# A Hymba block: the subtractions of the token pairs' mixing on GpSimd, and the second pair's scaling one group later

## The chip, the cores and the metric

The kernel runs on one core of a Trainium2 chip. The metric is the device time of one execution in microseconds (us). TensorE (PE) multiplies matrices, VectorE (DVE), ScalarE (ACT) and GpSimd (POOL) work elementwise, SyncE (SP) issues DMAs; GpSimd issues some as well. Each engine runs its own instructions in order and waits on semaphores for the others.

## What is computed

For x of 2048 tokens by 1024, in float32:

```python
h = _rmsnorm(x, norm1_w[layer])
proj = h @ w_in[layer]
qa, ka, va, qb, fb, ib, gb = jnp.split(proj, SPLIT_POINTS, axis=-1)
ya = _swa_sink_attention(qa, ka, va, q_norm_w[layer], k_norm_w[layer], attn_sinks[layer])
yb = _hgrn2(qb, fb, ib, gb, lower_bounds[layer], hgrn_gnorm_w[layer])
x = x + (jnp.concatenate([ya, yb], axis=-1) @ w_out[layer]).astype(x.dtype)
h = _rmsnorm(x, norm2_w[layer])
gate, up = jnp.split(h @ w_gate_up[layer], 2, axis=-1)
x = x + ((jax.nn.silu(gate) * up) @ w_down[layer]).astype(x.dtype)
```

`_hgrn2` is a gated linear recurrence over chunks of 64 tokens for four heads; its state between chunks is decayed and added to.

## The kernel before

Every product in float32 is made of three passes over a high and a low part (`three_passes`, L243 to L251): ScalarE copies a weight tile from its stage to `w_hi`, VectorE subtracts that from the stage for `w_lo` (L924).

The first phase (`build_phase_a`) takes the tokens in four blocks of 512. In a block the projections come in chunks of weight columns: KV, QA0, QA1, F0, F1, Q01, I01, G01, F23, Q23, I23, G23, and then WO0 to WO3 for the output projection. A chunk of 256 columns in token order has four groups (numbered 0 to 3) of 24 matmuls each; F and Q chunks have one group for each 128 columns. Two PSUM banks `pj` take turns, so that a group waits until the one before the last has been read. For the WO chunks VectorE reads it, by adding it to the residual tile `x_res` (L988).

The order of all other work is written by hand in `block_steps` (L73 to L143): `after(chunk, group, steps...)` hangs steps behind a group, and every engine walks the same list `STEPS` and does its own part of each step. For HGRN head h the steps are `ha`, `hb`, `hc` (gates), `kt`, `ds` (the update of the state, on VectorE at L1084 and L1088, whose last output is `a_carry`), `att`, `o` (TensorE, L902 and L907; waits for the state) and `on1` to `on3`, `yt` (norm and transposes; `on1` has a power on GpSimd, L513). `split_hi` and `split_lo` are the weight split of a later chunk.

The second phase multiplies the feed-forward matrices by a Strassen-like scheme, which wants seven combinations of each pair of token tiles, `hc` in DRAM. For the first half of the tokens these combinations, the *mixing*, are made in the last block of the first phase (block 3), from the rows of `x_mid` that earlier blocks have stored. A pair p of four is one step `("mix", p, 0)`, the scaling of two tiles of 128x1024 by the norm (L219), and one step `("mix", p, 1)`, four subtractions of 128x512 (L224 to L229). Both are VectorE's. There is one buffer `mix_x` and one `mix_t` for all pairs.

SyncE's queue holds the weight loads of all chunks (L444) and, at two places of that loop and behind it, `store_mixed` (L232 to L240; three stores, each waiting for its part on the semaphore `mixed`) and `load_mix` (L455 to L458), which waits until the pair before is stored. Pair 0 is stored and pair 1 loaded behind the load of G23 and ahead of that of WO0; pair 1 is stored and pair 2 loaded behind the load of WO1 and ahead of that of WO2; the rest comes behind all of them.

GpSimd's queue holds, beside the powers, the residual tiles: at the last group of each WO chunk it stores `x_res` to `x_mid` (L529, waits for ScalarE's squares), waits for that store, and loads the residual of a chunk two further on (L524).

Of the kernel before, what the change touches and what calls it, by code (L numbers as in the profile page):

```python
# [21 lines left out]
ALU = mybir.AluOpType  # L22
# [50 lines left out]
def block_steps():  # L73

    at = {}

    def after(name, group, *steps):
        at.setdefault((name, group), []).extend(steps)

    after("KV", 3, ("vmix",))
    after("QA1", 0, ("qn1", 0))
    after("QA1", 1, ("qn1", 1))
    after("QA1", 2, ("qn1", 2), ("qn2", 0))
    after("QA1", 3, ("qn1", 3))
    after("F0", 0, ("qn2", 1), ("split_hi", CHUNK_AT["Q01"]), ("split_lo", CHUNK_AT["Q01"]), ("qn2", 2))
    after("F1", 0, ("qn2", 3))
    after("Q01", 0, ("qT", 0), ("qT", 1), ("qT", 2), ("qT", 3), ("kT",))  # L90
    after("Q01", 1, ("sc", 0), ("sm1", 0), ("sm1", 1))
    after("I01", 0, ("ha", 0), ("split_hi", CHUNK_AT["G01"]))
    after("I01", 1, ("sm2", 0), ("sm2", 1), ("sc", 1), ("split_lo", CHUNK_AT["G01"]))
    after("I01", 2, ("pt", 0), ("pt", 1), ("sm1", 2), ("sm1", 3), ("hb", 0))
    after("I01", 3, ("sm2", 2), ("sm2", 3), ("pv", 0), ("sc", 2))
    after("G01", 0, ("pt", 2), ("pt", 3), ("sm1", 4), ("sm1", 5), ("xload",), ("hc", 0), ("ha", 1))
    after("G01", 1, ("sm2", 4), ("sm2", 5), ("pv", 1), ("split_hi", CHUNK_AT["F23"]), ("split_lo", CHUNK_AT["F23"]))
    after("G01", 2, ("pt", 4), ("pt", 5), ("sc", 3), ("att", 0), ("kt", 0), ("sm1", 6), ("sm1", 7), ("hb", 1))
    after("G01", 3, ("ds", 0, 0), ("ds", 0, 1), ("sm2", 6), ("sm2", 7), ("pv", 2), ("hc", 1))
    after("F23", 0, ("pt", 6), ("pt", 7))  # L100
    after("F23", 1, ("pv", 3), ("o", 0), ("on1", 0), ("kt", 1), ("ha", 2), ("sq", 0))
    after("Q23", 0, ("on2", 0), ("on3", 0), ("hb", 2), ("split_lo", CHUNK_AT["I23"]), ("ds", 1, 0), ("ds", 1, 1), ("att", 1))
    after("Q23", 1, ("yt", 0), ("hc", 2), ("sq", 1))
    after("I23", 0, ("o", 1), ("on1", 1), ("ha", 3))
    after("I23", 1, ("on2", 1), ("on3", 1), ("split_lo", CHUNK_AT["G23"]), ("kt", 2), ("sq", 2))
    after("I23", 2, ("yt", 1), ("att", 2), ("sq", 3))
    after("I23", 3, ("hb", 3),)
    after("G23", 0, ("ds", 2, 0), ("ds", 2, 1), ("hc", 3), ("n1a",))
    after("G23", 1, ("o", 2), ("on1", 2), ("kt", 3), ("n1b", 0), ("n1b", 1))
    after("G23", 2, ("on2", 2), ("ds", 3, 0), ("ds", 3, 1), ("att", 3))  # L110
    after("G23", 3, ("on3", 2), ("o", 3), ("on1", 3), ("yt", 2), ("n1b", 2), ("on2", 3), ("on3", 3), ("n1b", 3))
    after("Q23", 1, ("mix", 0, 0))
    after("I23", 1, ("mix", 0, 1))
    after("I23", 3, ("mix", 1, 0))
    after("G23", 0, ("mix", 1, 1))
    for n in range(CHUNK_AT["WO0"], NW):
        after(chunk_name(n), 1, ("split_lo", n + 1))
    after("WO0", 2, ("mix", 2, 0), ("mix", 2, 1))
    after("WO1", 3, ("mix", 3, 0), ("mix", 3, 1))
    after("WO0", 0, ("xT", 0))  # L120
    after("WO0", 1, ("xT", 1))
    after("WO0", 2, ("xT", 2))
    after("WO1", 0, ("xT", 3))
    after("WO1", 2, ("xT", 4))
    after("WO2", 0, ("xT", 5))
    after("WO2", 2, ("xT", 6))
    after("WO3", 0, ("xT", 7))

    placed = [step for group in at.values() for step in group if step[0].startswith("split")]
    steps = []  # L130
    for n in range(NW):
        first_steps = [part for part in (("split_hi", n + 1), ("split_lo", n + 1)) if part not in placed]
        for g in range(chunk_groups(n)):
            if (chunk_name(n), g) == ("WO0", 0):
                first_steps.append(("yt", HG - 1))
            if g == 0 and (chunk_groups(n) < TT or chunk_name(n) == "WO0"):
                steps += first_steps
            steps.append(("proj", n, g))
            steps += at.pop((chunk_name(n), g), [])
            if g == 0 and not (chunk_groups(n) < TT or chunk_name(n) == "WO0"):  # L140
                steps += first_steps
    assert not at, at
    return steps  # L143
# [71 lines left out]
def mix_tokens(dve, x, t, rs, at, n2w, mixed, part):  # L215

    if part == 0:
        for two in range(2):
            last = dve.scalar_tensor_tensor(out=x[:, two, :], in0=x[:, two, :], scalar=rs[:, at + 4 * two:at + 4 * two + 1], in1=n2w[:], op0=ALU.mult, op1=ALU.mult)  # L219
            if two == 0:  # L220
                last.then_inc(mixed, 1)
    else:
        dve.drain()
        dve.tensor_tensor(t[:, 0, :], x[:, 1, 0:512], x[:, 0, 0:512], ALU.subtract)  # L224
        dve.drain()
        dve.tensor_tensor(x[:, 1, 0:512], x[:, 1, 512:D], x[:, 1, 0:512], ALU.subtract).then_inc(mixed, 1)
        dve.tensor_tensor(t[:, 1, :], x[:, 1, 512:D], t[:, 0, :], ALU.subtract)
        dve.drain()
        dve.tensor_tensor(t[:, 2, :], t[:, 1, :], x[:, 0, 512:D], ALU.subtract).then_inc(mixed, 1)  # L229
# [24 lines left out]
def build_phase_a(nc, ctx, dram, x_mid, hc, kept):  # L254
# [159 lines left out]
    mid_ready = signal("mid_ready", 1, 1)  # L414
    mix_in, n2w_in, rs_ready = sem("a_mix_in"), sem("a_n2w_in"), sem("a_rs_ready")
    mixed, hc_stored = sem("a_mixed"), sem("a_hc_stored")
    pool_waited, dve_waited = sem("pool_waited"), sem("dve_waited")
    pool_set, dve_set, act_set = sem("pool_set"), sem("dve_set"), sem("act_set")

# [65 lines left out]
    def _(pool):  # L485
# [35 lines left out]
        for b in range(NB):  # L521
# [9 lines left out]
            for step in STEPS:  # L531
# [3 lines left out]
                if kind == "vmix":  # L535
                    if b == NB - 1:
                        wait(mid_ready.sem, 2)
                        pool.drain()
                        pool.tensor_tensor(kept.rs[:, 0:8], mid_ms[:, 0:8], neg_half[:, 0:8], ALU.pow).then_inc(rs_ready, 1)

                    wait(kv_ready.sem, kv_ready.upto(b, TT))
                    pool.drain()
                    pool.tensor_copy(v_even[CHUNK:P, 0, :], v_even[CHUNK:P, TT, :])
                    pool.drain()
                    pool.tensor_copy(v_even[0:CHUNK, 0:TT, :], v_nat[0:CHUNK, :, :])
                    pool.drain()
                    pool.tensor_copy(v_even[CHUNK:P, 1:TT + 1, :], v_nat[CHUNK:P, :, :]).then_inc(v_even_ready.sem, 1)
                elif kind == "qn1":
                    t = step[1]
                    power(q_rs[:, t, :], q_ss[:, t, :], SLOTS, q_ms_ready, q_rs_ready, q_ms_ready.upto(b, t + 1))  # L550
                elif kind == "sc" and step[1] == 1:

                    wait(sink_less_ready.sem, sink_less_ready.upto(b, 2))
                    pool.drain()
                    pool.memset(penalty[:], 0.0)
                elif kind == "xload":

                    wait(kT_full.sem, kT_full.upto(b, 1))
                    if b < NB - 1:
                        load_block(b + 1)  # L560
                    load_res(0)
                    load_res(1)
                elif kind == "on1":
                    h = step[1]
                    power(o_rs[:], o_ss[:], TT, o_ms_ready, o_rs_ready, o_ms_ready.upto(b, h + 1))
                elif kind == "n1a":
                    power(x_rs[:], ss[:], TT, ms_ready, x_rs_ready, ms_ready.upto(b, 1))
                elif kind == "proj" and chunk_name(step[1]).startswith("WO") and step[2] == TT - 1:
                    c = step[1] - len(CHUNKS)
                    store_res(c)  # L570


                    wait(xr_stored[c % 2], b * 32 + 16 * (c // 2 + 1))
                    if c < 2:
                        load_res(c + 2)
# [343 lines left out]
    def _(dve):  # L919
# [54 lines left out]
        for b in range(NB):  # L974
            use = 0
            for step in STEPS:
# [130 lines left out]
                    low_part(yH_lo[h][:], tr[use % 2][:], gnw[:, 0:1], yH_hi[h][:], yH_ready)  # L1107
                elif kind == "n1a":
                    mean_square_x(b)
                elif kind == "mix":  # L1110
                    p, part = step[1:]
                    if part == 0:
                        if p == 0:
                            dve.wait_ge(rs_ready, 1)
                            dve.wait_ge(n2w_in, 16)
                        dve.wait_ge(mix_in, 16 * (p + 1))
                    mix_tokens(dve, mix_x, mix_t, kept.rs, p, n2w, mixed, part)
                elif kind == "n1b":
                    scale_x(b, step[1])
                elif kind == "xT":  # L1120
# [738 lines left out]
```

## Time and profile before

| | us |
|---|---|
| median of 3 runs | 2197.1 |
| lowest and highest | 2196.92, 2197.79 |
| the profiled execution, its time | 2197.5 |
| its span | 2195.7 |
| TensorE busy | 2139.9 |
| VectorE busy | 1337.5 |
| ScalarE busy | 904.7 |
| GpSimd busy | 132.6 |

The span is that of the recorded instructions; the time has 1.8 us more around it. Busy times are sums over the span. A row of the timeline has the start from the beginning of the span, the duration, the engine, the line, what is written and read, and in brackets how long the engine had been idle and what released it. The first phase ends at about 900 us, its last block starts at about 672 us.

### The profile page before, as it was taken

Reading aid. Unit: us, or ns where it says so; the run is one execution under the profiler, and the core shown is the slowest. Engines: PE = TensorE matmul, PEld = TensorE weight load, DVE = VectorE, ACT = ScalarE, POOL = GpSimd, SP = SyncE. Lnnn points to the kernel's source line nnn. Section 1 sums busy time; section 2 is a strip of 40 time slices with the busy share of each in tenths; the row PEclk is TensorE's granted clock in tenths of the full one; section 3 lists DMA queues with packets and bytes.
Section 4 is the critical chain, followed back from the end, with each engine's and each line's share of the span. In section 5 each row is a group of like instructions: output and inputs, shape, how many; then the busy total and the mean of one; then the engine's idle time right before and its main releaser. Section 6 shows DMA issues by size and latency. Waiting matters only on the chain.

```text
span 2195.7 us, 30926 instructions
## 1 busy us (share of the span) xinstructions
PE 2139.9 (97%) x12376; PEld 1856.1 (85%) x12376; DVE 1337.5 (61%) x1967; ACT 904.7 (41%) x1575; POOL 132.6 (6%) x138
## 2 busy tenths in 40 slices
PE   7999999999999998799999999999999999999999
PEld 7889988998899888788888888888888888888887
DVE  4675367636753677567777667777777764444432
ACT  4774377437733762433323334333233332222221
POOL 2101110120012000100000000000000000000000
PEclk9999999999999999899999999999999999999999
DMA  3322232223223326634445335554444575645532
GB/s 138 136 78 91 102 136 78 97 97 139 75 97 105 136 82 237 229 117 141 156 152 187 101 115 187 177 191 140 164 155 146 181 253 175 214 166 179 186 132 91
DMA packets 156271, 316.22 MB, mean 144 GB/s; under 512 B 9504, under 2 KB 96800, under 8 KB 140128
## 3 DMA queue, kind: packets, MB, share of 16 engines
q1 hardware_dynamic: 144864, 265.74, 35.5%
q0 software_dynamic: 11264, 48.50, 6.1%
q8 instruction: 98, 1.61, 0.3%
q14 instruction: 45, 0.37, 0.1%
HBM read 230.85 MB, written 83.36 MB: 143 GB/s over the span
## 4 chain that ended last, share of the span: by engine, by line
PE 58%; DMA 0%; issue 0%; DVE 0%; POOLq 0%
PE b_bank_A L248 4%; PE b_bank_A L249 4%; PE b_bank_A L250 4%; PE b_bank_B L249 4%; PE b_bank_C L249 4%; PE b_bank_B L248 4%; PE b_bank_C L248 4%; PE b_bank_C L250 4%; PE b_bank_B L250 4%; PE b_hx_bank L1614 3%; PE b_hx_bank L1615 3%; PE b_hx_bank L1613 3%; PE b_bank_D L248 2%; PE b_bank_D L249 2%; PE b_bank_D L250 2%; PE b_hx_bank L1558 1%
## 5 line engine op out<-in xcount | busy, mean ns | idle before, releaser
L248 PE MATMUL a_pj<-a_w_hi,a_hT_hi 128*128 128x256 f32 x896 | 259.5, 290 | 1.7 <-issue 1.7
L249 PE MATMUL a_pj<-a_w_lo,a_hT_hi 128*128 128x256 f32 x896 | 253.6, 283 | 0.0
L250 PE MATMUL a_pj<-a_w_hi,a_hT_lo 128*128 128x256 f32 x896 | 253.6, 283 | 0.0
L1501 ACT ACTIVATE b_s_hi<-b_s_stage 128x1408 fp32r<-128x1408 f32 x56 | 77.4, 1382 | 300.1 <-PE b_hx_bank L1615 149.8
L924 DVE TENSOR_TENSOR a_w_lo<-a_w_stage,a_w_hi 128x2048 fp32r<-128x2048 f32 (+1 forms) x64 | 137.9, 2155 | 72.8 <-ACT a_w_hi L587 72.8
L248 PEld LDWEIGHTS a_pj<-a_w_hi,a_hT_hi 128*128 128x128 f32 x896 | 171.9, 192 | 6.7 <-issue 4.4
L249 PEld LDWEIGHTS a_pj<-a_w_lo,a_hT_hi 128*128 128x128 f32 x896 | 172.0, 192 | 0.0
L250 PEld LDWEIGHTS a_pj<-a_w_hi,a_hT_lo 128*128 128x128 f32 x896 | 171.8, 192 | 0.0
L248 PE MATMUL b_bank_A<-b_h_hi_B,b_w_hi 128*128 128x512 f32 x352 | 137.6, 391 | 0.0
L248 PE MATMUL b_bank_B<-b_h_hi_T,b_w_hi 128*128 128x512 f32 x352 | 137.3, 390 | 0.0
L250 PE MATMUL b_bank_A<-b_h_hi_B,b_w_lo 128*128 128x512 f32 x352 | 137.2, 390 | 0.0
L249 PE MATMUL b_bank_A<-b_h_lo_B,b_w_hi 128*128 128x512 f32 x352 | 137.2, 390 | 0.0
L250 PE MATMUL b_bank_B<-b_h_hi_T,b_w_lo 128*128 128x512 f32 x352 | 137.0, 389 | 0.0
L249 PE MATMUL b_bank_B<-b_h_lo_T,b_w_hi 128*128 128x512 f32 x352 | 137.0, 389 | 0.0
L1631 DVE TENSOR_TENSOR b_w_lo<-b_mixed_w,b_w_hi 128x1024 fp32r<-128x1024 f32 x88 | 107.5, 1222 | 22.1 <-ACT b_w_hi L1462 22.1
L1613 PE MATMUL b_hx_bank<-b_t_hi,b_s_hi 128*128 128x512 f32 x308 | 119.8, 389 | 0.0
L1614 PE MATMUL b_hx_bank<-b_t_lo,b_s_hi 128*128 128x512 f32 x308 | 119.8, 389 | 0.0
L1615 PE MATMUL b_hx_bank<-b_t_hi,b_s_lo 128*128 128x512 f32 x308 | 119.8, 389 | 0.0
L587 ACT ACTIVATE a_w_hi<-a_w_stage 128x2048 fp32r<-128x2048 f32 (+1 forms) x64 | 115.6, 1806 | 4.7 <-DMA a_w_stage<-w_whole 4.7
L1631 DVE TENSOR_TENSOR b_s_lo<-b_s_stage,b_s_hi 128x1408 fp32r<-128x1408 f32 x56 | 91.0, 1625 | 33.8 <-ACT b_s_hi L1501 32.7
L1522 ACT ACTIVATE b_s<-b_bank_C 128x512 f32<-128x512 f32 x44 | 26.4, 599 | 200.5 <-PE b_bank_C L250 200.5
L1538 ACT ACTIVATE b_gate<-b_u 128x512 f32<-128x512 f32 x44 | 27.8, 632 | 195.8 <-DVE b_u L1777 195.8
(280 smaller groups left out, 5526.9 us busy)
## 6 DMA issues: line engine op xcount, KB each, us to landing
a_w_stage<-w_whole SPq DMA_DIRECT2D x56, 1024.0 KB, 4.8
b_gu_stage<-w_gu SPq DMA_DIRECT2D x44, 1024.0 KB, 5.1
b_s_stage<-a_sums SPq DMA_DIRECT2D x56, 704.0 KB, 4.2
a_sums<-b_a SPq DMA_DIRECT2D x88, 256.0 KB, 5.5
a_sums<-b_gate SPq DMA_DIRECT2D x66, 256.0 KB, 4.1
b_hx<-hc POOLq DMA_DIRECT2D x13, 1024.0 KB, 5.3
b_w_blocks<-w_dn SPq DMA_DIRECT2D x11, 1024.0 KB, 4.7
a_x_res<-x_pad POOLq DMA_DIRECT2D x16, 512.0 KB, 5.4
```

The lines of the kernel that those rows point to most:

```text
L248: pe.matmul(out, stationary[0](k), moving[0](k), start=(k == 0 and not adds), stop=False, skip_group_check=adds)
L249: pe.matmul(out, stationary[0](k), moving[1](k), start=False, stop=False, skip_group_check=adds)
L250: last = pe.matmul(out, stationary[1](k), moving[0](k), start=False, stop=(k == ends), skip_group_check=adds)
L587: act.activation(w_hi[s][:, :, 0:cols], w_stage[s][:, :, 0:cols], ACT.Copy).then_inc(w_hi_ready.sem, 1)
L924: dve.tensor_tensor(w_lo[s][:, :, 0:cols], w_stage[s][:, :, 0:cols], w_hi[s][:, :, 0:cols].bitcast(F32), ALU.subtract).then_inc(w_lo_ready ...
L1501: act.activation(f.s_hi[n % 2][:], f.s_stage[n % 2][:], ACT.Copy).then_inc(f.s_hi_ready, 1)
L1522: act.activation(f.s5[:], f.bank["C"][:], ACT.Copy).then_inc(f.s5_ready, 1)
L1538: act.activation(f.gate[1][:], f.u2[:], ACT.Silu).then_inc(f.silu_ready[1], 1)
L1613: pe.matmul(out, s_hi[:, k, :], t_hi, start=(k == 0 and not adds), stop=False, skip_group_check=adds)
L1614: pe.matmul(out, s_hi[:, k, :], t_lo, start=False, stop=False, skip_group_check=adds)
L1615: last = pe.matmul(out, s_lo[:, k, :], t_hi, start=False, stop=(k == PAIRS_FF - 1), skip_group_check=adds)
L1631: dve.tensor_tensor(out, full, hi.bitcast(F32), ALU.subtract).then_inc(ready, 1)
```

## The change

The four subtractions of each pair in the last block of the first phase become GpSimd's, with a drain between them; GpSimd waits for the scaling by a new semaphore `mix_scaled`. The step of pair 0's subtractions goes from behind group 1 of I23 to behind group 0, pair 1's scaling from behind group 3 of I23 to behind group 0 of G23, at the end of that list, and pair 1's subtractions from behind group 0 of G23 to behind group 3. Pairs 2 and 3 keep their places. The mixing of the second half of the tokens, in the second phase, stays VectorE's.

```diff
--- before.py
+++ after.py
@@ -110,9 +110,9 @@
     after("G23", 2, ("on2", 2), ("ds", 3, 0), ("ds", 3, 1), ("att", 3))
     after("G23", 3, ("on3", 2), ("o", 3), ("on1", 3), ("yt", 2), ("n1b", 2), ("on2", 3), ("on3", 3), ("n1b", 3))
     after("Q23", 1, ("mix", 0, 0))
-    after("I23", 1, ("mix", 0, 1))
-    after("I23", 3, ("mix", 1, 0))
-    after("G23", 0, ("mix", 1, 1))
+    after("I23", 0, ("mix", 0, 1))
+    after("G23", 0, ("mix", 1, 0))
+    after("G23", 3, ("mix", 1, 1))
     for n in range(CHUNK_AT["WO0"], NW):
         after(chunk_name(n), 1, ("split_lo", n + 1))
     after("WO0", 2, ("mix", 2, 0), ("mix", 2, 1))
@@ -219,6 +219,7 @@
             last = dve.scalar_tensor_tensor(out=x[:, two, :], in0=x[:, two, :], scalar=rs[:, at + 4 * two:at + 4 * two + 1], in1=n2w[:], op0=ALU.mult, op1=ALU.mult)
             if two == 0:
                 last.then_inc(mixed, 1)
+        return last
     else:
         dve.drain()
         dve.tensor_tensor(t[:, 0, :], x[:, 1, 0:512], x[:, 0, 0:512], ALU.subtract)
@@ -414,6 +415,7 @@
     mid_ready = signal("mid_ready", 1, 1)
     mix_in, n2w_in, rs_ready = sem("a_mix_in"), sem("a_n2w_in"), sem("a_rs_ready")
     mixed, hc_stored = sem("a_mixed"), sem("a_hc_stored")
+    mix_scaled = sem("a_mix_scaled")
     pool_waited, dve_waited = sem("pool_waited"), sem("dve_waited")
     pool_set, dve_set, act_set = sem("pool_set"), sem("dve_set"), sem("act_set")
 
@@ -560,6 +562,17 @@
                         load_block(b + 1)
                     load_res(0)
                     load_res(1)
+                elif kind == "mix" and step[2] == 1:
+                    x, t = mix_x, mix_t
+                    pool.drain()
+                    pool.wait_ge(mix_scaled, step[1] + 1)
+                    pool.tensor_tensor(t[:, 0, :], x[:, 1, 0:512], x[:, 0, 0:512], ALU.subtract)
+                    pool.drain()
+                    pool.tensor_tensor(x[:, 1, 0:512], x[:, 1, 512:D], x[:, 1, 0:512], ALU.subtract).then_inc(mixed, 1)
+                    pool.drain()
+                    pool.tensor_tensor(t[:, 1, :], x[:, 1, 512:D], t[:, 0, :], ALU.subtract)
+                    pool.drain()
+                    pool.tensor_tensor(t[:, 2, :], t[:, 1, :], x[:, 0, 512:D], ALU.subtract).then_inc(mixed, 1)
                 elif kind == "on1":
                     h = step[1]
                     power(o_rs[:], o_ss[:], TT, o_ms_ready, o_rs_ready, o_ms_ready.upto(b, h + 1))
@@ -1107,14 +1120,13 @@
                     low_part(yH_lo[h][:], tr[use % 2][:], gnw[:, 0:1], yH_hi[h][:], yH_ready)
                 elif kind == "n1a":
                     mean_square_x(b)
-                elif kind == "mix":
-                    p, part = step[1:]
-                    if part == 0:
-                        if p == 0:
-                            dve.wait_ge(rs_ready, 1)
-                            dve.wait_ge(n2w_in, 16)
-                        dve.wait_ge(mix_in, 16 * (p + 1))
-                    mix_tokens(dve, mix_x, mix_t, kept.rs, p, n2w, mixed, part)
+                elif kind == "mix" and step[2] == 0:
+                    p = step[1]
+                    if p == 0:
+                        dve.wait_ge(rs_ready, 1)
+                        dve.wait_ge(n2w_in, 16)
+                    dve.wait_ge(mix_in, 16 * (p + 1))
+                    mix_tokens(dve, mix_x, mix_t, kept.rs, p, n2w, mixed, 0).then_inc(mix_scaled, 1)
                 elif kind == "n1b":
                     scale_x(b, step[1])
                 elif kind == "xT":
```

## Rows read from the trace of the kernel before

**Rows 1.** The head of the page, and its chain that ended last.

```profile
span 2195.7 us, 30926 instructions
...
PE 58%; DMA 0%; issue 0%; DVE 0%; POOLq 0%
```

**Rows 2.** TensorE's waits from 780 to 1000 us: us in total, times, longest.

```profile
PE a_hb L902 <- DVE a_carry L1088: 7.7, 1, 7.7
```

**Rows 3.** Timeline of VectorE, last block: start, us, instruction, idle time before it.

```profile
811.54 0.69 DVE L224 TENSOR_TENSOR a_mix_t<-a_mix_x 128x512 f32<-128x512 f32 x1
...
817.80 0.69 DVE L1035 TENSOR_TENSOR a_k_end<-a_t_b 128x512 f32<-128x512 f32 x1
823.02 2.48 DVE L219 SCALAR_TENSOR_TENSOR a_mix_x<-a_mix_x,rs,a_n2w 128x1024 f32<-128x1024 f32 x2 [4.54 <-DMA a_mix_x<-x_mid]
...
829.01 0.35 DVE L1088 SCALAR_TENSOR_TENSOR a_carry<-a_state,a_decay,a_tr 128x128 f32<-128x128 f32 x1
...
834.77 2.29 DVE L924 TENSOR_TENSOR a_w_lo<-a_w_stage,a_w_hi 128x2048 fp32r<-128x2048 f32 x1
...
838.26 0.69 DVE L1098 TENSOR_TENSOR a_y_nat<-a_hb,a_o_rs 128x512 f32<-128x512 f32 x1 [1.12 <-POOL a_o_rs L513]
...
856.67 2.47 DVE L219 SCALAR_TENSOR_TENSOR a_mix_x<-a_mix_x,rs,a_n2w 128x1024 f32<-128x1024 f32 x2
```

**Rows 4.** Timeline of TensorE, last block.

```profile
817.58 1.16 PE L895 MATMUL a_tr<-a_i_nat,a_k_nat 64*128 64x128 f32 x16
...
829.50 2.04 PE L902 MATMUL a_hb<-a_i_nat,a_att_m 128*128 128x128 f32 x8 [7.70 <-DVE a_carry L1088]
...
843.46 1.16 PE L902 MATMUL a_hb<-a_i_nat,a_att_m 128*128 128x128 f32 x8 [0.37 <-DVE a_att_m L1080]
...
862.43 0.39 PE L248 MATMUL a_pj<-a_w_hi,a_yA_hi 128*128 128x256 f32 x1 [0.38 <-DVE a_x_res L988]
...
877.47 0.39 PE L248 MATMUL a_pj<-a_w_hi,a_yA_hi 128*128 128x256 f32 x1 [0.39 <-DVE a_x_res L988]
```

**Rows 5.** Stretches: us, busy of PE, PEld, DVE, ACT, POOL, granted clock, DMA, GB/s.

```profile
385.00:403.00 18.00, 15.89 (x150) 14.56 (x149) 13.30 (x27) 5.95 (x23) 4.47 (x2) 1.00 0.17 59
...
822.00:829.50 7.50, 0.00 (x0) 0.03 (x1) 5.54 (x12) 2.86 (x4) 0.00 (x0) 0.74 0.96 371
829.50:834.00 4.50, 4.50 (x27) 3.94 (x28) 4.26 (x7) 0.50 (x4) 0.00 (x0) 0.50 0.02 5
```

**Rows 6.** GpSimd's groups, shapes apart: busy us, mean ns of one.

```profile
L513 POOL TENSOR_TENSOR a_q_rs<-a_q_ss,a_neg_half 128x10 f32<-128x10 f32 x16 | 38.5, 2408 | 66.6 <-DVE a_q_ss L994 66.3 <-issue 0.3
...
L547 POOL COPY a_v_even<-a_v_nat 64x512 f32<-64x512 f32 x4 | 2.5, 613 | 0.5
```

**Rows 7.** Timeline of GpSimd, block 1 and last block.

```profile
390.26 2.98 POOL L513 TENSOR_TENSOR a_x_rs<-a_ss,a_neg_half 128x4 f32<-128x4 f32 x1 [18.22 <-DVE a_ss L928]
...
806.09 1.24 POOL L513 TENSOR_TENSOR a_o_rs<-a_o_ss,a_neg_half 128x4 f32<-128x4 f32 x1 [18.11 <-DVE a_o_ss L1094]
...
847.11 1.01 POOL L513 TENSOR_TENSOR a_o_rs<-a_o_ss,a_neg_half 128x4 f32<-128x4 f32 x1 [8.89 <-DVE a_o_ss L1094]
863.51 0.81 POOL L529 DMA_DIRECT2D x_mid<-a_x_res  x1 [15.40 <-ACT a_junk L640]
869.24 0.75 POOL L524 DMA_DIRECT2D a_x_res<-x_pad  x1 [4.92 <-DMA x_mid<-a_x_res]
```

**Rows 8.** Timelines of SyncE's queue and of ScalarE, last block.

```profile
814.40 0.36 SPq L240 DMA_DIRECT2D hc<-a_mix_t  x1
818.25 0.36 SPq L458 DMA_DIRECT2D a_mix_x<-x_mid  x1
818.66 0.93 SPq L444 DMA_DIRECT2D a_w_stage<-w_whole  x2
...
826.00 1.91 ACT L587 ACTIVATE a_w_hi<-a_w_stage 128x2048 fp32r<-128x2048 f32 x1 [3.32 <-DMA a_w_stage<-w_whole]
```

**Rows 9.** DMA issues of the page: count, size, median us to landing.

```profile
a_x_res<-x_pad POOLq DMA_DIRECT2D x16, 512.0 KB, 5.4
```

## The prediction

> **What bounds the kernel now.** I read the head of the page first: the profiled execution has a span of 2195.7 us and took 2197.5 us, 0.4 above the median of the runs (2197.1), and the chain that ended last runs over TensorE (PE) [rows 1]. So another engine's work counts only where TensorE stands still for it. The list of TensorE's waits from 780 us on has one large entry in the last block: 7.7 us for `a_carry`, the state update of HGRN head 2 [rows 2]. VectorE's timeline says why that update was late [rows 3]. VectorE finished the step `hb` of head 3 at 818.5 (row 817.80), then came pair 1's scaling: it waited 4.54 us for its tokens, ran 823.02 to 825.5, and only then came the update, over at 829.4. The products that the update adds had been there since 818.7 (row 817.58), and TensorE stood from 821.8 to 829.50 [rows 4]. The stall was paid twice: the granted clock averaged 0.74 over 822 to 829.5 and 0.50 (the 1.2 GHz level) over 829.5 to 834, while block 1, whose waits there are short, kept 1.00 (2.4 GHz) over 385 to 403 [rows 5]. Work of 4.5 us done at half clock is worth 2.3, so stall and clock hold some 10 us, the most that there is to win.
>
> **What the change removes.** (a) Pair 1's scaling goes behind the update and behind head 3's `hc`. The update can start at 818.7; it took 3.9 (825.5 to 829.4), so the state is ready at 822.6 and TensorE starts `o` of head 2 at 822.7, not 829.5. (b) Sixteen subtractions of 0.69 leave VectorE (row 811.54), four in each pair: 2.8 us a pair.
>
> **What it adds: the price of a GpSimd subtraction.** No row has one of 128x512. The same subtraction on VectorE, 0.69, is the low end; the longest usual two-input instruction of GpSimd, a power of 128x10, takes 2.4 and is the high end; its copy with one input, 64x512, takes 0.61 [rows 6]. I take twice the copy, 1.2, as there are two operands to read and the power's cost is not that of reading; with gaps of 0.1 four cost 5.2, against 2.8 on VectorE. The Trainium skill ("GPSIMD Engine Reference", Performance versus the Vector engine) gives 2.6 cycles an element at 1.2 GHz for this kind; 512 of them would be an estimated 1.11 us plus dispatch. No run here shows it yet.
>
> **Do the two engines wait for each other?** In block 1 a power of 128x4 took 2.98 us, beside a weight split of VectorE; the same shape took 1.01 when alone (row 847.11) [rows 7]. So GpSimd does lose time to a VectorE instruction, here 2.0; whether VectorE loses time to GpSimd no row shows, so I bound that by nothing and by one subtraction each time. I take turns both ways. The skill ("SBUF — State Buffer", Who interferes with whom) states such a rule: an exclusive lock between a GpSimd instruction that reads SBUF and a VectorE one with two SBUF inputs. By it the sum is the one below, without it the first rival.
>
> **Pair 0.** GpSimd is free from the power at 807.3 [rows 7]; alone the four would end at 812.5. The VectorE work queued there holds a 0.7 product and a 2.3 split (the split is 834.77 to about 837 in the later copy), so I add 3.0: 815.6, which is 1.2 later than the issue of the last store at 814.40 [rows 8]. VectorE's turns behind GpSimd cost it about what it is spared (2.8), so its `hb` still ends near 818.5. SyncE is next: its stores, `load_mix` of pair 1 and, behind that, the weights of WO0 are one queue. The load of pair 1 goes out at 819.4 (was 818.25) and lands 4.8 later (818.25 to 823.02), at 824.2; the WO0 weights go out at 819.9 and land 7.3 later (818.66 to 826.0), at 827.2, and ScalarE's high part takes 1.9 [rows 8]: 829.1.
>
> **From the update to head 3's `o`.** VectorE after 822.6: `hc` of head 3, 2.6 (829.4 to 834.77 less four subtractions), to 825.2; scaling 2.5, to 827.7, its tokens there since 824.2; then it waits for the high part until 829.1. From the split's start to the scaled `y_nat` of head 2 it took 3.5 (834.77 to 838.26), so 832.6, and to TensorE's `o` of head 3 another 5.2 (to 843.46): 837.8. Gain here: 5.7 us. The short waits of TensorE in between are in that figure.
>
> **Pair 1, where I expect part of it to be given back.** Its subtractions now stand behind head 3's power, which moves with TensorE from 847.11 to 841.4 and ends at 842.4. Four at 5.2 and one turn of 0.7 end at 848.3 (VectorE had done this by about 834.9). Pair 2's tokens are loaded behind the last store: 3.85 (814.40 to 818.25) and 4.8, so 857.0. VectorE reaches pair 2's scaling at 856.67 - 5.7 = 851.0 and now waits 6.0 us for it. Behind it stand the residual additions that free the projection banks, and for these TensorE waits. Before, scaling and subtractions held VectorE 5.3 us and cost TensorE 0.38 at 862.43. Now TensorE starts WO1's group 1 at 857.0 + 2.5 + 0.5 = 860.0: 2.4 ahead of before, 3.3 given back, after a wait of 3.6. SyncE's loads of WO2 and WO3 also go out behind this, near 852.6, and land by 859.9; a group takes 2.93 (five groups from 862.43 to 877.47), so the WO2 split is not wanted before 862.9: covered.
>
> **Pair 2 on GpSimd's queue.** Its four run 859.5 to 864.7. Behind them in the same queue is the store of the first residual tile (was 863.51), so 864.7; then the 5.7 us to the load (863.51 to 869.24) and its landing after 5.4 [rows 7, 9]: 875.8. VectorE's add and TensorE's WO2 group 2 follow at 876.3, before it was 877.47 [rows 4]. What is left is 1.2 us.
>
> **Pair 3.** GpSimd has the second residual load out by about 878 and subtracts after it, to about 883; stores and the first `b_hx` load follow near 887. TensorE's first phase ends six groups after 876.3, near 894, so this and the later stores are covered; if the cover went, each late microsecond would move the whole second phase. The WO3 split meets pair 3's subtractions and may end 1 us late against a start of WO3 at 882: nothing, with up to 0.5 as bound. The second phase is TensorE's own chain and only shifts.
>
> **The sum.** 5.7 gained, 3.3 and 1.2 given back: 1.2 us faster than the profiled execution, 2196.3, or 2195.9 on the median's scale. I say 2196.0. What a measurement here can tell from no change is about 0.2%, 4.4 us.
>
> **Rivals.** First, no turns (0.26): GpSimd's pairs cost 5.2 and nothing else. WO0's weights land before they are asked for, the split starts at 827.7, `o` of head 3 at 836.4 (7.1 ahead). Pair 1 ends at 846.2, pair 2's tokens are there at 854.8, WO1's group 1 starts at 857.8, pair 2's subtractions end at 862.5, WO2's group 2 starts at 874.1: 3.4 faster, 2194.0. With the low end, 0.69, each four takes 2.0 less, nothing waits for GpSimd, and the first gain stays: 7 faster, 2190. For it: VectorE never shows such a wait. Against it: the power of 2.98.
>
> Second, slower (0.22): GpSimd's subtraction becomes the bound of the output projection. Three fours stand in series on the way (pair 0 to WO0's weights, pair 1 to pair 2's tokens, pair 2 to the residual load), so every 0.1 us more costs 1.2 in all. Break-even is 1.3 us; at 1.5 the sum is 2.4 slower, and TensorE's waits at WO1 group 1 and WO2 group 2 grow past 4 us. If the clock is then granted at half, as after 821.8, the stretch from 829.5 to 834 gives its price, 2.3 us or more: 2202 to 2203. At the high end, 2.4, it is 14.4 - 1.2 = 13 slower, 2210. For it: 3.6 us lies between block 1's waits, which left the clock at 1.00, and the 7.7 after which it was at 0.50. Against it: at 1.2 nothing reaches 1.5.
>
> Third (0.06): the moved scaling doesn't free the update, because GpSimd's turns hold up `hb` of head 3 and pair 0 ends beyond 818; then the stall shrinks by only 3 or so and pair 1's loss remains: 2198, no change to be seen.
>
> **How the numbers follow.** My own case has 0.46 and lies between 2193 and 2199. Faster by over 0.2% (below 2192.7) is the first rival wherever the subtraction is under 1.1, some two thirds of it: 0.18. Slower (above 2201.5) is most of the second: 0.20. Within: 0.62. For 8 in 10 the range takes the first rival well towards its low end, 2191.0, and the second's 2203 with a little over: 2204.0.
>
> **What would show it.** In the profile after: TensorE's 7.7 us wait for `a_carry` down to about 1, with no stretch of clock 0.50 at 829; subtractions of some 1.2 on GpSimd, stretched beside weight splits; a new wait of VectorE, some 6 us, for `a_mix_x` of pair 2; TensorE waits for `a_x_res` of 3.6 and 1.6; a later first residual load. I am wrong if the subtractions take 0.8 or less or over 1.5, if VectorE doesn't wait for pair 2's tokens, or if the clock falls in the output projection.

## The result, and the profile after

The changed kernel takes 2203.1 us in the median of 9 runs (2201.6 to 2205.2), beside 2197.4 for the kernel before (2196.9 to 2197.8): the ratio is 1.0027, with an interval of 1.0018 to 1.0036. It is slower by some 6 us, where I had forecast 2196.0 and no change to be seen. The profiled execution took 2201.56 us, the fastest of the nine, so that its trace shows 4.1 us of loss and not all of it.

The head of its page: span, and TensorE's busy time.

```profile
span 2199.8 us, 30930 instructions
...
PE 2142.5 (97%) x12376; PEld 1858.4 (84%) x12376; DVE 1330.8 (60%) x1951; ACT 904.8 (41%) x1575; POOL 155.8 (7%) x154
```

TensorE's waits from 780 to 1000 us (us in total, times, longest), to be read against [rows 2]:

```profile
PE a_pj L249 <- DVE a_x_res L1001: 6.0, 3, 3.0
...
PE a_tr L908 <- ACT a_k_nat L733: 2.3, 1, 2.3
PE a_hb L888 <- DVE a_y_nat L1111: 1.3, 1, 1.3
PE a_hb L915 <- DVE a_carry L1101: 0.7, 1, 0.7
PE a_tr L896 <- DVE a_q_h L1057: 0.5, 1, 0.5
```

The 7.7 us for `a_carry` are gone, as forecast; what is left is 0.7. But TensorE waits again, twice for `a_x_res`, the residual additions (2.8 and 3.0 us), and before that 2.3 and 1.3 us for head 3's transpose and for `y_nat`.

GpSimd's timeline, which answers to [rows 7]:

```profile
807.70 1.30 POOL L569 TENSOR_TENSOR a_mix_t<-a_mix_x 128x512 f32<-128x512 f32 x1 [0.16 <-issue]
...
810.86 3.15 POOL L573 TENSOR_TENSOR a_mix_t<-a_mix_x,a_mix_t 128x512 f32<-128x512 f32 x1 [0.16 <-issue]
...
846.23 1.54 POOL L571 TENSOR_TENSOR a_mix_x<-a_mix_x 128x512 f32<-128x512 f32 x1
...
867.03 0.81 POOL L531 DMA_DIRECT2D x_mid<-a_x_res  x1
872.92 0.76 POOL L526 DMA_DIRECT2D a_x_res<-x_pad  x1 [5.08 <-DMA x_mid<-a_x_res]
```

A subtraction costs 1.29 us. The third of pair 0 took 3.15: it stood behind VectorE's weight split. The turns go both ways, as VectorE's timeline shows (it answers to [rows 3]): the same split, 2.29 before, took 3.38 beside GpSimd.

```profile
809.47 3.38 DVE L937 TENSOR_TENSOR a_w_lo<-a_w_stage,a_w_hi 128x2048 fp32r<-128x2048 f32 x1
...
829.29 2.29 DVE L937 TENSOR_TENSOR a_w_lo<-a_w_stage,a_w_hi 128x2048 fp32r<-128x2048 f32 x1 [1.59 <-ACT a_w_hi L600]
...
832.78 0.69 DVE L1111 TENSOR_TENSOR a_y_nat<-a_hb,a_o_rs 128x512 f32<-128x512 f32 x1 [1.12 <-POOL a_o_rs L515]
...
858.95 2.48 DVE L219 SCALAR_TENSOR_TENSOR a_mix_x<-a_mix_x,rs,a_n2w 128x1024 f32<-128x1024 f32 x2 [5.22 <-DMA a_mix_x<-x_mid]
...
875.85 2.48 DVE L219 SCALAR_TENSOR_TENSOR a_mix_x<-a_mix_x,rs,a_n2w 128x1024 f32<-128x1024 f32 x2 [3.20 <-DMA a_mix_x<-x_mid]
880.47 0.75 DVE L1001 TENSOR_TENSOR a_x_res<-a_x_res,a_pj 128x256 f32<-128x256 f32 x2 [2.13 <-DMA a_x_res<-x_pad]
```

Then two waits of VectorE that the kernel before doesn't have: 5.2 us for pair 2's tokens (858.95), and 3.2 us for pair 3's (875.85). Last, the residual tile of WO2, whose load GpSimd issues at 872.92, lets VectorE add only at 880.47, 2.1 us after pair 3's scaling was done. SyncE's queue, which answers to [rows 8]:

```profile
819.46 0.36 SPq L460 DMA_DIRECT2D a_mix_x<-x_mid  x1
...
867.12 0.36 SPq L241 DMA_DIRECT2D hc<-a_mix_t  x1
870.68 0.36 SPq L460 DMA_DIRECT2D a_mix_x<-x_mid  x1
871.08 0.50 SPq L480 DMA_DIRECT2D b_gu_stage<-w_gu  x1
```

And TensorE itself: two matmuls behind its waits of 2.3 and 1.3 us, then head 3's `o`, WO1 group 1 and WO2 group 2, beside 843.46, 862.43 and 877.47 before [rows 4]:

```profile
835.89 0.41 PE L251 MATMUL a_pj<-a_w_hi,a_hT_lo 128*128 128x256 f32 x1
836.10 0.41 PE L249 MATMUL a_pj<-a_w_hi,a_hT_hi 128*128 128x256 f32 x1
...
840.06 1.05 PE L915 MATMUL a_hb<-a_i_nat,a_att_m 128*128 128x128 f32 x8
...
861.81 0.39 PE L249 MATMUL a_pj<-a_w_hi,a_yA_hi 128*128 128x256 f32 x1 [2.79 <-DVE a_x_res L1001]
...
880.94 0.58 PE L249 MATMUL a_pj<-a_w_hi,a_yA_hi 128*128 128x256 f32 x1 [2.99 <-DVE a_x_res L1001]
```

TensorE is 3.4 us ahead at `o`, 0.6 ahead at WO1 group 1, and 3.5 behind at WO2 group 2. The matmuls near 836 start 0.21 us apart, and 0.12 apart from 839.5 on. The granted clock of four stretches (it stands behind the busy times, ahead of the DMA share), which answers to [rows 5]:

```profile
829.50:834.00 4.50, 1.54 (x18) 1.41 (x19) 3.31 (x5) 1.82 (x11) 1.01 (x1) 0.84 0.09 32
834.00:850.00 16.00, 15.50 (x112) 14.52 (x111) 7.67 (x17) 4.60 (x12) 5.79 (x5) 0.83 0.09 31
...
860.00:865.00 5.00, 3.19 (x20) 3.19 (x21) 2.09 (x4) 2.83 (x5) 3.19 (x3) 0.83 0.99 354
...
880.00:885.00 5.00, 4.06 (x23) 4.06 (x24) 2.49 (x3) 2.71 (x5) 0.75 (x1) 0.66 0.62 234
```

It fell after each group of waits, and no wait here was longer than 3.0 us.

### The profile page after: what moved, and what is told of

Read it like the earlier page. It is cut to its first block, busy times and chain, and to the rows that moved or that the text cites. A ratio compares the mean times of both kernels' runs of the same rounds, so it can differ in the third digit from the quotient of the medians.

```text
span 2199.8 us, 30930 instructions
## 1 busy us (share of the span) xinstructions
PE 2142.5 (97%) x12376; PEld 1858.4 (84%) x12376; DVE 1330.8 (60%) x1951; ACT 904.8 (41%) x1575; POOL 155.8 (7%) x154
## 4 chain that ended last, share of the span: by engine, by line
PE 58%; DMA 0%; issue 0%; DVE 0%; POOLq 0%
PE b_bank_A L249 4%; PE b_bank_B L249 4%; PE b_bank_C L249 4%; PE b_bank_B L251 4%; PE b_bank_A L251 4%; PE b_bank_C L251 4%; PE b_bank_A L250 4%; PE b_bank_C L250 4%; PE b_bank_B L250 4%; PE b_hx_bank L1626 3%; PE b_hx_bank L1625 3%; PE b_hx_bank L1627 3%; PE b_bank_D L249 2%; PE b_bank_D L251 2%; PE b_bank_D L250 2%; PE b_hx_bank L1570 1%
```

## The experiments

All times are medians; the kernel before ran beside each on the same chip, at 2197.3 to 2197.5 us. Four questions were asked: the places or the engine (e1, e2), which wait (e3, e8, e9), which pair (e5, e6, e7), and what the clock is worth (e4, e11). Two more look for a better version (e10, e12). They ran in three sets, each on another chip: e1 to e4; e6 to e9; e5 and e10 to e12. The changed kernel's 2203.1 is that of the first section. An interval reaches 0.1%, some 2 us, to each side, so a difference of 2 us or less between two experiments is likely and not sure.

The profiled executions aren't all typical of their kernels. Those of the changed kernel, e3, e5, e9 and e12 were 1.5 to 2.4 us faster than the median, those of e2 and e4 0.9 and 0.5 slower. Starts read from two traces compare no finer than that; the waits within one trace are sounder.

### e1: the places alone

The three `after(...)` lines of the change, put into the kernel before; VectorE subtracts.

> The new positions of the steps, all of the mixing on VectorE. My theory (the loss comes from pair 2's tokens being loaded late, behind subtractions that were put late and made slow, and from TensorE's clock falling in the waits that follow): the a_carry wait of 7.7 us shrinks to under 1, VectorE still waits for pair 2's tokens, some 4 to 5 us instead of 5.2, nothing is queued on GpSimd, so the first residual load is where it was. About 2196 to 2200 us, that is 3 to 7 faster than the changed kernel. Rival (the late place alone makes the whole loss, GpSimd costs nothing): within 1 us of the changed kernel, 2202 or more. Rival (GpSimd is all of the loss): 2190 or less, as the stall of 10 us is won in full.

2197.8 us, ratio 0.9999 (0.9991 to 1.0008): no change, as my theory had it. VectorE waits 2.9 us for pair 2's tokens (I had 4 to 5), and TensorE waits for VectorE at WO1 group 1:

```profile
861.15 0.58 PE L248 MATMUL a_pj<-a_w_hi,a_yA_hi 128*128 128x256 f32 x1 [3.37 <-DVE a_x_res L988]
```

Its granted clock there, in the same columns as above:

```profile
860.00:865.00 5.00, 3.85 (x18) 3.85 (x19) 1.35 (x3) 2.82 (x5) 0.81 (x1) 0.55 1.04 401
```

TensorE was 5.5 us ahead of the kernel before at head 3's `o` (837.98), 1.3 ahead at WO1 group 1, and 1.4 behind at WO2 group 2 (878.89). The last 2.7 are the clock's: there is no wait at WO2 group 2 beyond the 0.4 of before, but from WO1 group 1 to WO2 group 2 it took 17.7 us and not 15.0.

### e2: the engine alone

```diff
-    after("I23", 0, ("mix", 0, 1))
-    after("G23", 0, ("mix", 1, 0))
-    after("G23", 3, ("mix", 1, 1))
+    after("I23", 1, ("mix", 0, 1))
+    after("I23", 3, ("mix", 1, 0))
+    after("G23", 0, ("mix", 1, 1))
```

(against the changed kernel)

> The subtractions on GpSimd, every step in its old position. My theory: pair 1's scaling again stands ahead of the state update and its tokens come 1.2 us later than before, so the a_carry wait is about 9 us; pair 2's tokens are loaded near 836, long before they are wanted, so no wait of VectorE for them; VectorE is spared 2.8 us a pair. Within 2 us of the kernel before: 2195.5 to 2199. Rival (GpSimd's slower subtractions and the turns they take with VectorE are the loss themselves): 2201 or more.

2203.4 us, ratio 1.0027 (1.0016 to 1.0038). My expectation failed and the rival's number came: with the old places the engine alone loses as much as the whole change. The wait for `a_carry` was 8.6 us (I had about 9), and VectorE didn't wait for pair 2's tokens, as expected; the loss comes later. The trace says where. GpSimd's timeline and SyncE's queue:

```profile
864.40 1.30 POOL L575 TENSOR_TENSOR a_mix_t<-a_mix_t,a_mix_x 128x512 f32<-128x512 f32 x1
865.64 0.81 POOL L531 DMA_DIRECT2D x_mid<-a_x_res  x1
872.16 0.76 POOL L526 DMA_DIRECT2D a_x_res<-x_pad  x1 [5.71 <-DMA x_mid<-a_x_res]
```

```profile
865.73 0.36 SPq L241 DMA_DIRECT2D hc<-a_mix_t  x1
871.97 0.36 SPq L460 DMA_DIRECT2D a_mix_x<-x_mid  x1
```

Pair 2's last subtraction releases two things at once: SyncE stores pair 2 (865.73), and GpSimd, whose queue it had held up, stores the first residual tile (865.64). Each waits for its own store before it loads: pair 3's tokens go out at 871.97, 6.2 us after the store where the kernel before needed 3.5 (862.07 to 865.60), and the residual at 872.16. With the next weights at 872.37 three loads then start within 0.4 us. VectorE can add 9.7 us after the residual load's issue (881.90), and TensorE's WO2 group 2 starts at

```profile
882.38 0.58 PE L249 MATMUL a_pj<-a_w_hi,a_yA_hi 128*128 128x256 f32 x1 [5.08 <-DVE a_x_res L1001]
```

4.9 us later than before (877.47), after a wait of 5.1. Before, VectorE's own subtractions let SyncE store pair 2 at 862.07, and nothing of them stood in GpSimd's queue.

### e3: pair 1's subtractions behind group 1 of G23

```diff
-    after("G23", 3, ("mix", 1, 1))
+    after("G23", 1, ("mix", 1, 1))
```

> The changed kernel with pair 1's subtractions hung behind group 1 of G23 instead of group 3, so that they run near 833 to 838. My theory: pair 2's tokens land near 847, VectorE's 5.2 us wait and TensorE's 2.8 at WO1 group 1 go, pair 2's own subtractions start 5 us sooner and the residual load no longer holds WO2 group 2; 6 us of TensorE's waits and the clock lost behind them. 2193 to 2196 us. Rival (GpSimd's queue holds the residual load whatever pair 1 does): the wait of 3.0 at WO2 group 2 stays, 2198 to 2200. Rival (the loss is in the stretch before 850): no gain, 2202 or more.

2198.3 us, ratio 1.0003 (0.9994 to 1.0012): 4.8 faster than the changed kernel, though not the 2193 to 2196 that I expected. Pair 2's tokens are there in time and the wait at WO1 group 1 is gone. The wait at WO2 group 2 is not: it is 3.6 us, and the time is that of the first rival. But it isn't the residual load that ends it in this trace. VectorE waits 6.0 us for pair 3's tokens, scales them, and adds without any further wait:

```profile
872.62 2.48 DVE L219 SCALAR_TENSOR_TENSOR a_mix_x<-a_mix_x,rs,a_n2w 128x1024 f32<-128x1024 f32 x2 [6.02 <-DMA a_mix_x<-x_mid]
875.01 0.74 DVE L1001 TENSOR_TENSOR a_x_res<-a_x_res,a_pj 128x256 f32<-128x256 f32 x2
```

### e4: the clock kept up

```diff
+        def keep_warm(count, s):
+            for i in range(count):
+                pe.matmul(sc[0][:, 0:WC], hT_hi[:, i % KT, 0:P], w_hi[s][:, i % KT, :], start=True, stop=True)
...
+                    if h == 3 and b == NB - 1:
+                        keep_warm(8, 1)
```

> The changed kernel with matrix multiplies added whose results nobody reads, ahead of four of TensorE's waits in the last block (16 before ds of head 3, 8 before att of head 3, 20 before WO1 group 1, 20 before WO2 group 2; 128x256, some 0.12 us each, less than each wait lasts). If the clock that falls in the waits costs what the granted clock of the stretches says (some 6.8 us of work lost in the changed kernel from 829 to 885), the time falls by 3 to 6 us, to 2197 to 2200, with the granted clock near 1.00 throughout, and the spread between runs shrinks. Rival (the clock is only a sign, or its loss is hidden in the next wait): within 1 us of the changed kernel.

2202.8 us, ratio 1.0025 (1.0015 to 1.0034): nothing gained, the rival's number and not mine. Timelines of TensorE and GpSimd:

```profile
859.35 0.39 PE L249 MATMUL a_pj<-a_w_hi,a_yA_hi 128*128 128x256 f32 x1 [0.46 <-DVE a_x_res L1011]
...
881.33 0.58 PE L249 MATMUL a_pj<-a_w_hi,a_yA_hi 128*128 128x256 f32 x1 [4.92 <-DVE a_x_res L1011]
```

```profile
863.37 3.16 POOL L575 TENSOR_TENSOR a_mix_t<-a_mix_t,a_mix_x 128x512 f32<-128x512 f32 x1
```

The clock was 1.00 from 829.5 to 865, and WO1 group 1 starts 2.5 us sooner than in the changed kernel. So the falls before it had been on the way to it. WO2 group 2 nevertheless starts 0.4 later, after a wait of 4.9 instead of 3.0. Two things take back what the clock had given. TensorE's earlier group lets VectorE start the split of WO2 sooner (862.87 for 866.53), and pair 2's last subtraction now meets it and takes 3.16 us instead of 1.28; the residual store goes out only 0.55 us sooner than in the changed kernel (866.48). And its load, issued at 872.34, lets VectorE add 8.5 us later (7.5 in the changed kernel). This point hangs on the chain of GpSimd, the stores and the loads. Nor was the clock kept behind it: over 880 to 885 it was 0.50 (0.66 in the changed kernel). So e4 is no clean price of the clock.

### e5, e6, e7: pairs 2 and 3 back on VectorE

In all three, on the changed kernel (e5), on e3 (e6) and on e2 (e7), VectorE subtracts pairs 2 and 3 and GpSimd the other two:

```diff
-                elif kind == "mix" and step[2] == 1:
+                elif kind == "mix" and step[2] == 1 and step[1] < 2:
```

> The changed kernel with its own places of the steps, pairs 2 and 3 subtracted on VectorE again. It keeps the late subtractions of pair 1 and takes pair 2 off GpSimd's queue. Theory (two causes that hide each other: pair 2's tokens late, and pair 2's subtractions ahead of the residual store): VectorE is now held 5.2 + 2.5 + 2.8 us at WO0 group 2, so TensorE waits 5 to 6 us at WO1 group 1 and hardly at WO2 group 2; little is gained, 2199 to 2203. Rival (GpSimd's queue alone makes the loss): 2194 or less, as in e6.

> As e3 (pair 1's subtractions behind group 1 of G23, on GpSimd), and pairs 2 and 3 subtracted on VectorE again. Theory: what costs time is that pair 2's subtractions stand in GpSimd's queue ahead of the first residual tile's store, and end at the same moment as they release the store of pair 2, so that residual load, pair 3's tokens and other transfers crowd. Without that the stretch of the output projection is the one of the kernel before, moved forward by the 5 us won before it: 2191 to 2194 us, no wait of TensorE over 1 us after 850. Rival (late or slow mixing of pairs 0 and 1 still spoils the rest): 2196 or more.

> As e2 (every step in its old place), with pairs 2 and 3 subtracted on VectorE again, pairs 0 and 1 on GpSimd. Theory: of e2's 6 us of loss 5 belong to pair 2 and only 1 to the later tokens of pair 1, so 2197 to 2199 us. Rival (the loss of e2 lies with GpSimd's subtractions of pairs 0 and 1, or in the second phase): 2201 or more.

| kernel | places | GpSimd subtracts | us | ratio (interval) |
|---|---|---|---|---|
| changed | new | all | 2203.1 | 1.0027 (1.0018 to 1.0036) |
| e1 | new | none | 2197.8 | 0.9999 (0.9991 to 1.0008) |
| e5 | new | pairs 0, 1 | 2200.5 | 1.0011 (1.0002 to 1.0020) |
| e2 | old | all | 2203.4 | 1.0027 (1.0016 to 1.0038) |
| e7 | old | pairs 0, 1 | 2197.6 | 1.0000 (0.9991 to 1.0009) |
| e3 | pair 1 early | all | 2198.3 | 1.0003 (0.9994 to 1.0012) |
| e6 | pair 1 early | pairs 0, 1 | 2192.2 | 0.9978 (0.9969 to 0.9987) |
| e10 | pair 1 early | none | 2194.1 | 0.9983 (0.9974 to 0.9991) |

All three came as expected. Pairs 2 and 3 on GpSimd cost 2.6 us in the changed kernel's places and 5.8 and 6.1 in the other two (e2 less e7, e3 less e6). No run separates pair 2 from pair 3; that pair 2 makes the loss is read from the traces, where pair 3's subtractions come after WO2 group 2. In e5 VectorE is held for tokens, scaling and subtractions together, so TensorE loses at WO1 group 1 what it no longer loses at WO2 group 2:

```profile
861.56 0.58 PE L249 MATMUL a_pj<-a_w_hi,a_yA_hi 128*128 128x256 f32 x1 [5.70 <-DVE a_x_res L1001]
...
879.32 0.39 PE L249 MATMUL a_pj<-a_w_hi,a_yA_hi 128*128 128x256 f32 x1 [0.40 <-DVE a_x_res L1001]
```

Between the two it took 17.8 us for 15.0, with no wait of note: as in e1, the clock, 0.59 over 860 to 865, costs 2.7 in the open. In e6 neither wait is left. Its list of TensorE's waits, without those at the border of the phases and two under 1 us:

```profile
PE a_tr L908 <- ACT a_k_nat L733: 2.3, 1, 2.3
PE a_hb L888 <- DVE a_y_nat L1111: 1.3, 1, 1.3
PE a_pj L249 <- DVE a_x_res L1001: 1.0, 3, 0.4
```

### e8, e9: the residual tiles loaded early

In the last block the tiles of WO2 and WO3 get memory that the attention has finished with, and are loaded there ahead of the output projection.

```diff
+                elif kind == "sc" and step[1] == 3 and b == NB - 1:
+                    wait(sc_full.sem, sc_full.upto(b, 8))
+                    for c in (2, 3):
+                        pool.dma_start(last_res[c - 2][:], x_cols[b:b + 1, :, :, c, :].rearrange("o p t n -> p (o t) n")).then_inc(last_loaded, 16)
```

> The changed kernel, where in the last block the residual tiles of WO2 and WO3 have memory of their own and are loaded early, ahead of the output projection, so that no load waits for GpSimd's queue, for the subtractions of pair 2 or for a store. Theory: the wait of 3.0 us at WO2 group 2 goes (or shrinks to the 0.5 that pair 3's scaling leaves) with the clock lost behind it, the one at WO1 group 1 stays: 2197 to 2200 us. Rival (pair 3's tokens, late as well, hold VectorE and by it TensorE): 2201 or more.

> e3 and e8 together: pair 1's subtractions early, the residual tiles of WO2 and WO3 loaded early, all subtractions on GpSimd. If the residual load is the one thing that holds WO2 group 2 in e3, its wait of 3.6 us goes and the time is 2192 to 2194. If pair 3's tokens hold it (VectorE waited 6.0 us for them in e3, and its next addition stands behind that), it is 2195 to 2198.

e8: 2199.1 us, 1.0011 (1.0002 to 1.0020), 4.1 faster than the changed kernel and inside what I expected. e9: 2195.3 us, 0.9988 (0.9979 to 0.9996), 3.0 faster than e3 and in the second of my two cases: VectorE waits 4.4 us for pair 3's tokens there, and TensorE 1.9 at WO2 group 2. In e8 the wait at WO2 group 2 is 1.6 instead of 3.0 (I had at most 0.5), and it is pair 3's scaling on VectorE that ends it:

```profile
860.53 0.58 PE L249 MATMUL a_pj<-a_w_hi,a_yA_hi 128*128 128x256 f32 x1 [2.93 <-DVE a_x_res L1014]
...
878.29 0.39 PE L249 MATMUL a_pj<-a_w_hi,a_yA_hi 128*128 128x256 f32 x1 [1.61 <-DVE a_last_res L1014]
```

So in the changed kernel the residual load ends that wait, but only 1.4 of its 3.0 us go with it: pair 3's late tokens stand right behind. By the medians the early residual tiles are worth 3.0 of the 6.1 us between e3 and e6, and 3.1 (e9 less e6) stay with pairs 2 and 3 on GpSimd.

### e10, e11, e12: from e6 on

e10 is e6 with everything on VectorE. e11 is e6 with the matrix multiplies of e4 ahead of the two waits before 834. e12 is e6 with SyncE's queue turned round:

```diff
-                if b == NB - 1 and n in (CHUNK_AT["G23"], CHUNK_AT["WO0"] + 1):
-                    p = 0 if n == CHUNK_AT["G23"] else 1
+                if b == NB - 1 and n in (CHUNK_AT["WO0"], CHUNK_AT["WO0"] + 1):
+                    p = n - CHUNK_AT["WO0"]
```

> The places of e6 (pair 0's subtractions behind group 0 of I23, pair 1's scaling behind group 0 of G23, its subtractions behind group 1), everything on VectorE. It says whether GpSimd is of any use. Theory: VectorE is behind in this stretch, so each subtraction on it lengthens the way to head 3's o; 1 to 3 us slower than e6, 2193 to 2196. Rival (the place of pair 1's scaling is the whole gain): the same as e6 within 1 us.

> e6 with 16 and 8 matrix multiplies whose results nobody reads ahead of the waits at ds and att of head 3. In e4 the same was given back at WO2 group 2; in e6 nothing stands there to take it. The granted clock of e6 over 829.5 to 850 was 0.92, which is 1.6 us of work: 1 to 2 us faster than e6, 2190 to 2191.5. Rival (the lower clock costs nothing real): e6 within 0.5 us.

> e6 with one more edit: on SyncE's queue the weights of WO0 are loaded ahead of pair 0's stores and pair 1's load, no longer behind them. Theory: ScalarE's high part of WO0 and with it head 3's transpose (TensorE waited 2.3 us for it at ds) are no longer late, VectorE's split starts 1.6 us sooner: 2 to 3 us faster than e6, 2189 to 2190.5, and the clock stays at 1.00 after 829. Rival (VectorE's own chain holds att, the transfers were hidden): under 1 us.

e10: 2194.1 us, 1.8 behind e6, as expected, though the two intervals overlap. So GpSimd is probably worth something for pairs 0 and 1, where VectorE is behind; in e10 TensorE stood 3.7 us at head 3's `att` (e6: 1.3):

```profile
834.78 1.57 PE L875 MATMUL a_hb<-a_q_in,a_f_gate 128*128 128x128 f32 x6 [3.69 <-DVE a_y_nat L1098]
```

e11: 2192.6 us, 0.9977 (0.9967 to 0.9986). I expected 1 to 2 us less than e6 and got none. The clock was at 1.00 where e6 had 0.92 over 829.5 to 850, yet `o` of head 3 started at 838.61 against 838.93, now waiting for VectorE:

```profile
829.50:834.00 4.50, 3.98 (x39) 3.52 (x38) 3.32 (x4) 2.08 (x12) 1.83 (x2) 1.00 0.14 51
834.00:850.00 16.00, 14.91 (x126) 13.95 (x127) 9.83 (x19) 5.51 (x16) 5.31 (x5) 1.00 0.56 214
```

```profile
838.61 1.16 PE L923 MATMUL a_hb<-a_i_nat,a_att_m 128*128 128x128 f32 x8 [0.72 <-DVE a_att_m L1101]
```

```profile
838.93 1.05 PE L915 MATMUL a_hb<-a_i_nat,a_att_m 128*128 128x128 f32 x8
```

e12: 2190.6 us, 0.9968 (0.9956 to 0.9980), the fastest of all: 6.7 us under the kernel before and 12.5 under the changed one. I had expected 2 to 3 us less than e6, and got 1.6; the clock was 1.00 over 829.5 to 850, as expected. The interval of these six runs overlaps that of e6, so the 1.6 is a likely size and not a sure one. ScalarE's high part of WO0, which in the changed kernel let the split start at 829.29, is done at 823.6, and the split starts when VectorE is ready for it:

```profile
821.65 1.91 ACT L600 ACTIVATE a_w_hi<-a_w_stage 128x2048 fp32r<-128x2048 f32 x1
```

```profile
827.11 2.28 DVE L937 TENSOR_TENSOR a_w_lo<-a_w_stage,a_w_hi 128x2048 fp32r<-128x2048 f32 x1
```

## Why the prediction was wrong

**The stall** ("so the state is ready at 822.6"): right. TensorE started head 2's `o` at 822.75.

**The subtraction's price** ("twice the copy, 1.2"): nearly right, 1.29. The Trainium skill ("GPSIMD Engine Reference", Performance versus the Vector engine) leads to the estimate of 1.11 plus dispatch. The trace agrees as far as it can: 1.29 leaves 0.18 for the dispatch, which no run here shows by itself. Four took 5.6 where I had 5.2.

**The turns**: right both ways. The lock that the Trainium skill states ("SBUF — State Buffer", Who interferes with whom) is borne out by the 3.15 of a subtraction and the 3.38 of a split. Pair 0's last store went out at 815.65 (I had 815.6), pair 1's load at 819.46 (819.4), the split at 829.29 (829.1), `y_nat` at 832.78 (832.6).

**To head 3's `o`** ("837.8. Gain here: 5.7 us"): the gain was 3.4. I took 5.2 us from `y_nat` to `o` and it was 7.3. Between them TensorE's matmuls started 0.21 us apart up to 839.3; in the trace before, those of the same group (from 839.98) started 0.12 apart; the granted clock of the two stretches was 0.84 and 0.83. It had fallen behind waits of 2.3 and 1.3 us of which I had counted each as harmless. This term stood in the forecast with no clock at all.

**Pair 1** ("Now TensorE starts WO1's group 1 at ... 860.0"): right in kind, 861.81: 1.8 late, because head 3's power, pair 1's subtractions and pair 2's tokens all follow `o`. The wait was 2.8, not 3.6, since TensorE came later.

**Pair 2 on GpSimd's queue**: this is the step that failed most. I wrote that the load follows at 870.4 "and its landing after 5.4", and gave TensorE's group 2 at 876.3. It started at 880.94, 4.6 later. Of this 2.0 were there already when pair 2's subtractions began (861.51 for 859.5); 0.5 came from the four subtractions and the store; and 2.1 from the landing, as VectorE could add 7.5 us behind the load's issue. I had moved the queue's entries one by one at the durations of a trace where they were apart. But the last subtraction is the common release of two stores, and these of two loads, and in the changed kernel both loads and the next weights start between 870.68 and 872.92 (before, 865.60 to 869.24).

The same step had no term at all for pair 3's tokens, whose load waits for pair 2's store. VectorE waited 3.2 us for them, and in e8, without the late residual, they still hold TensorE 1.6 us. What I called "covered" were pair 3's own subtractions and stores, and those were: the second phase is late by little more than WO2 group 2.

The sizes: pairs 2 and 3 as the only edit are worth 5.8 and 6.1 us (e2 less e7, e3 less e6), but 2.6 in the changed kernel's own places (e5), where VectorE, held by pair 2's late tokens, loses the rest at WO1 group 1. e8 and e9 give the residual load 4.1 and 3.0. That the crowd of transfers, and not some other delay, stretches the landing is not shown. The DMA engines were busy all the time from 873 to 880.5, but so they were from 869.3 to 877 in the kernel before. And e8 and e9, which take the residual load out of the crowd, don't agree: pair 3's tokens land 5.2 us behind their issue in the changed kernel and in e8, but 5.9 in e3 and 4.8 in e9.

**The clock**: my second rival had it fall in the output projection, for subtractions of 1.5 us; it fell at 1.29, and that was one of my own signs of being wrong. After the 2.8 and the 3.0 us the granted clock was 0.83 and 0.66. From WO2 group 2 to the second phase's first transposes the kernel before took 23.4 us and this one 24.3: 0.9 for the last fall, on TensorE's own chain. The fall before `o` cost 2.1, and it moved WO1 group 1, as e4 shows (2.5 us sooner without it). The fall behind WO1 group 1 cost 1.5 us of TensorE's time, but TensorE then waited 3.0 us at WO2 group 2 all the same, so it was hidden; in e1 and e5, where no such wait follows, it cost 2.7 in the open. The rival's number, 2202 to 2203, was that of the result, but its way (1.5 us a subtraction, then the clock) was only in part the one taken. I gave it 0.22 and my own case 0.46. That 2203.1 lies inside my range of 2191 to 2204 is no merit of the forecast: the upper end was taken from this rival.

**The sum**: forecast 5.7 - 3.3 - 1.2 = +1.2 gained. The trace: 3.4 at `o`, 2.8 given back to WO1 group 1, 4.1 to WO2 group 2, 0.9 behind it: 4.4 lost, where the two spans differ by 4.1. Between forecast and trace lie 5.6 us: 1.8 at WO1 group 1, nearly all of it from the clock behind the two short waits; 2.9 between there and WO2 group 2, pair 2's step; 0.9 for the clock behind it. What the other runs lose beyond that, some 1.6 us in the median, no trace shows. The spreads don't tell either. The changed kernel's nine runs lie 3.6 us apart and the nine of the kernel before 0.9, but in the three later sets 27 to 33 runs of the kernel before lie 3.1 to 3.5 apart. This stays open.

## What to carry to other kernels

When work is moved to an engine that also issues DMAs, price the DMAs behind it first: here pairs 0 and 1 cost nothing on GpSimd (e7, e6), and pairs 2 and 3, ahead of the residual store and load and of pair 3's tokens, up to 6 us. When one instruction releases two chains of store and load, their loads go out together, and durations taken from a trace where they were apart may not hold (5.4 us became 7.5, 8.5 and 9.7). And a wait that is taken away shows its worth only if the next one is moved as well: the new places alone gave nothing (e1), the engine for pairs 0 and 1 alone nothing (e7), pair 1 early in the new places 3.2 us (e10), and that with the engine for pairs 0 and 1 5.1 (e6). Last, a fallen clock cost nothing here where a wait followed that another engine ended, and its full price where none did (e1, e5).

## What the runs showed of the hardware

TensorE's granted clock (1.00 is 2.4 GHz, and what lies below it a mixture with 1.2 GHz) came down after waits much shorter than the 7.7 us of before: it was 0.84 over 829.5 to 834, behind waits of 2.3 and 1.3 us, 0.83 over 860 to 865 behind one of 2.8, and 0.66 over 880 to 885 behind one of 3.0. In e1 it was 0.55 over 860 to 865 behind one of 3.4, and the way to WO2 group 2 took 2.7 us longer. With the waits filled by multiplies that nobody reads it was 1.00 over 829.5 to 850 (e11), and that was worth nothing where another engine ended the stretch.

GpSimd's subtraction of 128x512 took 1.29 us, and 3.15 and 3.16 where it met a weight split of VectorE; that split, 2.29 otherwise, took 3.38 where GpSimd's subtraction had started first.
